# Weight tiles of an encoder kernel stored interleaved in pairs and loaded with a step of 8 bytes

## The chip, the core and the metric

The kernel runs on one core of one Trainium2 chip. The time is device microseconds of one execution of the whole program. TensorE (PE) has two granted clocks here, 1.2 and 2.4 GHz; the profile writes them as 0.5 and 1.00. PEld in the profile is TensorE's weight load (LDWEIGHTS), PE its matmul.

## The reference

One step of a streaming encoder of two layers, for 512 new frames and 64 frames of a running stream, 576 columns (tokens) in all, with a model width of 1024:

```
for i in range(2):
    x = x + 0.5 * swiglu(rmsnorm(x), ffn1_w_in[i], ffn1_w_out[i])      # 1024 -> 2 x 2816 -> 1024
    u = rmsnorm(x)
    y = pool_mixer(u) if i == 0 else mlstm_mixer(u)                    # causal pooling / matrix memory
    x = x + y
    x = x + 0.5 * swiglu(rmsnorm(x), ffn2_w_in[i], ffn2_w_out[i])
y = rmsnorm(x)
```

Beside y the states of both mixers are returned. All inputs are float32. The four SwiGLU blocks are nearly all of the arithmetic.

## The kernel before

**The products.** Every large product is done as three float32r matmuls of one weight tile of 128x128: high part of the weights by high part of the data, high by low, low by high. `passes(u, kk, m_h, m_l)` (L1829) gives these three pairs in this order for tile `kk` of unit `u`. The matmul's stationary operand, which PEld loads, is the weight tile: 128 partitions, 128 float32 columns. The moving operand is 288 columns of data, half of the 576 tokens (`HALF`). No load serves two matmuls: each matmul has its own LDWEIGHTS of 128 columns, issued as the matmul ahead of it starts.

**Four FFNs, each in two phases.** In a phase `ffn_in` runs the products into the hidden layer (`product_mm`, matmuls recorded at L1850), 77 products of 4 tiles x 3 passes on sums and differences of the blocks, held in `u7`; then `ffn_out` runs the products back (`block_mm`, recorded at L1840), 8 output tiles of 11 weight tiles x 3 passes x 2 halves on `h_hi` and `h_lo`. The mLSTM projections (`project`) use `block_mm` too, on `um_hi` and `um_lo`.

**The weights' way.** A DMA brings a unit into a raw buffer (`raw_x`, `raw_y`, `raw_z`, `w_raw`, ...). ACT copies it rounded to float32r into `w_hi` (L726), DVE writes the remainder into `w_lo` (L1231), both contiguous, at `PLACE[u]` in a ring of 8 entries of 4 tiles (2048 bytes in a partition). PE frees an entry by `unit_used`. Of the units of an output tile one has 6 weight tiles and one 5 (`OUT_UNIT`); the pool mixer reads its weights as moving operand (L2032), and the gates are a unit of their own.

**Addresses in a partition.** From the sizes in the code, taken modulo 256 bytes: `w_hi` 128 (address 120192), `w_lo` 128 (136576), the high pieces of `u7` 0 and the low pieces 128, `h_hi`, `h_lo`, `um_hi`, `um_lo` 0 at the first half and 128 at the second, since a half is 1152 bytes, 4.5 times 256. A weight tile is 512 bytes, so every tile begins at its tensor's residue.

Of the kernel before, what the change touches and what calls it, by code (L numbers as in the profile page):

```python
# [3 lines left out]
P = 128  # L4
D_MODEL = 1024
DT = D_MODEL // P
# [5 lines left out]
FT = D_FF // P  # L12
PAIRS = FT // 2
# [13 lines left out]
ENTRY = 4 * P  # L27
RING = 8
OUT_UNIT = (6, 5)
# [101 lines left out]
AT, KEYS, PLACE, LEAVES, RAW_AFTER, SLOT, TURN = unit_tables()  # L131
# [3 lines left out]
def encoder_step(nc, a):  # L135
    F32, F32R = mybir.dt.float32, mybir.dt.float32r
# [5 lines left out]
    def region(size):  # L142
        offset = place[0]
        place[0] += (size + 63) // 64 * 64
        assert place[0] <= nc.sbuf_usable_end, place[0]
        return offset

    def sb(name, shape, dt=F32, at=None):
        size = 4
        for s in shape[1:]:  # L150
            size *= s
        return nc.alloc_sbuf_tensor_at(name, shape, dt, offset=region(size) if at is None else at)
# [4 lines left out]
    def align(size, residue=0):  # L157
        place[0] += (residue - place[0]) % size
# [18 lines left out]
    raw_z = [sb(f"raw_z{s}", [P, ENTRY], at=raw_at + (2 + s) * ENTRY * 4) for s in range(2)]  # L177
    raw_y = [sb(f"raw_y{s}", [P, ENTRY], at=raw_at + (4 + 2 * s) * ENTRY * 4) for s in range(2)]
    raw_x = [sb(f"raw_x{s}", [P, ENTRY], at=raw_at + (5 + 2 * s) * ENTRY * 4) for s in range(2)]
    w_hi, w_lo = sb("w_hi", [P, RING * ENTRY], F32R), sb("w_lo", [P, RING * ENTRY], F32R)  # L180
    rstd = sb("rstd", [P, TOK])
    rows_at = region(4 * TOK * 4)
    tmp = sb("tmp", [P, 2, TOK], at=rows_at)
# [240 lines left out]
    with block as block:  # L424
# [111 lines left out]
        def _(pool):  # L536
# [122 lines left out]
            for c in range(NB):  # L659
                _, n = block_cols(c)  # L660
                pool.wait_ge(scale_ready, c // 2 + 1)
                pool.tensor_tensor(v_one[0:n, c, :, 0:DV], v_one[0:n, c, :, 0:DV],
                                   dd[0:n, c, :].unsqueeze(2).to_broadcast([n, HEADS, DV]), ALU.mult) \
                    .then_inc(h_scaled, 1)
# [15 lines left out]
        def _(act):  # L680
# [403 lines left out]
            for j in range(DT):  # L1084
                middle, _ = IN_O[j]
                if j == 5:
                    variance_root(1)
                if middle and middle[0] == "vt":
                    item("vt", 7, ITEM_AT[8])
                elif middle:  # L1090
                    c = middle[1]
                    _, L = block_cols(c)
                    act.wait_ge(out_read, c + 1)
                    for h in range(HEADS):
                        last = act.activation(junk[0:L, :], v_one[0:L, c, h, 0:DV], ACT.Square,
                                              accum_out=ssum[0:L, c, h:h + 1])
                        if h < HEADS - 1:
                            last.then_inc(act_order, 1)
                            order += 1
                            act.wait_ge(act_order, order)  # L1100
                    last.then_inc(squares, 1)
                if j == 3:
                    variance_root(0)
                if j < DT - 1:
                    ahead(U_M + 17 + j)
                else:
                    y_high(0)
                if j == 5:
                    variance_root(2)
                act.wait_ge(proj_read, 18 + j + 1)  # L1110
                act.activation(og[:, j, :], og[:, j, :], ACT.Sigmoid).then_inc(og_ready, 1)
# [92 lines left out]
        def _(dve):  # L1204
# [451 lines left out]
            def chunk(kind, c):  # L1656

                _, L = block_cols(c)
                old, new = old_state(c)
                if kind == "upd":  # L1660
                    dve.wait_ge(upd_psum, c + 1)
                    if c == 0:
                        dve.wait_ge(q_scaled, NB - 1)
                        dve.tensor_copy(c_st[new][:, :, :], ps[:, 4:8, 0:DV + 1]).then_inc(state_ready, 1)
                        return
                    if c == NB - 1:
                        dve.wait_ge(state_landed, 16)
                    else:
                        dve.wait_ge(state_ready, c)
                    for h in range(HEADS):  # L1670
                        last = dve.scalar_tensor_tensor(
                            c_st[new][:, h, :], c_st[old][:, h, :],
                            carry[:, c - 1:c, h], ps[:, 4 + h, 0:DV + 1], ALU.mult, ALU.add)
                    last.then_inc(state_ready, 1)
                elif kind == "out":
                    dve.wait_ge(out_psum, c + 1)
                    dve.tensor_copy(v_one[0:L, c, :, :], ps[0:L, 4:8, 0:DV + 1]).then_inc(out_read, 1)
# [150 lines left out]

        @block.tensor  # L1829
        def _(pe):  # L1830
            def passes(u, kk, m_h, m_l):

                w = slice(PLACE[u] + kk * P, PLACE[u] + (kk + 1) * P)
                return (w_hi[:, w], m_h), (w_hi[:, w], m_l), (w_lo[:, w], m_h)

            def block_mm(u, kk, k, bank, first, last):

                for p, (w, m) in enumerate(passes(u, kk, *k)):
                    for h in range(2):
                        mm = pe.matmul(ps[:, bank + h, 0:HALF], w, m[:, h * HALF:(h + 1) * HALF],  # L1840
                                       start=first and p == 0, stop=last and p == 2)
                return mm

            def product_mm(f, ph, prod, n, kp):

                u = f.unit(ph, prod, n)
                dst = r_bank(n) if prod in ("M5", "M3") else q_bank(f, ph, n) if prod == "M2" else p_bank(n)
                piece = PIECES.index(MOVING[prod])
                for p, (w, m) in enumerate(passes(u, kp, u7[:, kp, piece, 0, :], u7[:, kp, piece, 1, :])):
                    mm = pe.matmul(dst, w, m, start=prod in ("M1", "M2", "M5") and kp == 0 and p == 0,  # L1850
                                   stop=kp == KP - 1 and p == 2,
                                   skip_group_check=prod in ("M3", "M4", "M6", "M7"))
                if kp == KP - 1:
                    mm.then_inc(unit_used, 1)
# [371 lines left out]
            def last_half(h, first, end):  # L2226

                at = slice(h * HALF, (h + 1) * HALF)
                for k in range(first, end):
                    s, kk = (0, k) if k < OUT_UNIT[0] else (1, k - OUT_UNIT[0])  # L2230
                    u = ffn_d.unit(1, "out", DT - 1, s)
                    for p, (w, m) in enumerate(passes(u, kk, h_hi[:, k, at], h_lo[:, k, at])):
                        mm = pe.matmul(ps[:, out_bank(DT - 1) + h, 0:HALF], w, m, start=k == 0 and p == 0,  # L2233
                                       stop=k == PAIRS - 1 and p == 2, skip_group_check=True)
                if end == PAIRS:
                    mm.then_inc(half_out, 1)
# [128 lines left out]
```

## Time and profile before

| | |
|---|---|
| time, median of 3 runs | 1878.55 us (1876.36 to 1881.43) |
| the profiled execution | 1879.91 us, its span 1878.1 us |
| mean granted TensorE clock | 0.996 |
| PE, PEld busy | 99%, 98% of the span |
| DVE, ACT, POOL busy | 67%, 46%, 18% |
| DMA | 234.71 MB, 125 GB/s mean |

Matmuls overlap in the records: one of 288 columns is recorded as about 295 ns long, while the next starts after about 130 ns. So the record's length is not what one costs; the distance between starts is. It is read here from the timeline, where rows of matmuls alternate in their operands, or as a stretch divided by the matmuls that start in it.

### The profile page before, as it was taken

The numbers are of one execution on the slowest core, as the hardware profiler recorded it, in microseconds if no ns is written. First come the engines' busy times: TensorE is split into PE (matmuls) and PEld (weight loads), VectorE is DVE, ScalarE is ACT, GpSimd is POOL, SyncE is SP. The second block draws the span as 40 slices with busy tenths as digits, with TensorE's granted clock in tenths as the row PEclk, the third lists the DMA queues.
The fourth block names the chain that finished last, engine by engine and source line by source line (L and its number), as shares of the span: only waits on it lengthen the run. The fifth ranks groups of instructions, "written<-read, shape, count | busy, mean of one in ns | idle before, by whom it ended". The sixth has DMA issues, their size and how long they took to land.

```text
span 1878.1 us, 34441 instructions
## 1 busy us (share of the span) xinstructions
PE 1855.2 (99%) x13850; PEld 1834.6 (98%) x13850; DVE 1251.5 (67%) x1999; ACT 866.9 (46%) x1518; POOL 329.5 (18%) x352
## 2 busy tenths in 40 slices
PE   8999999999999999999999999999999999999998
PEld 8999999998999999999999999999989999999998
DVE  7874487668884488679853886563546888548853
ACT  7552355347552355346532553232334665235532
POOL 2220122131220122132201221300010322012112
PEclk9999999999999999999999999999999999999999
DMA  8773576334763576347644763231113576357632
GB/s 207 166 149 105 128 167 148 108 85 95 166 147 108 127 167 150 107 107 165 146 131 102 171 141 101 86 102 68 57 45 103 117 169 152 108 120 167 135 93 82
DMA packets 116830, 234.71 MB, mean 125 GB/s; under 512 B 13184, under 2 KB 15248, under 8 KB 116672
## 3 DMA queue, kind: packets, MB, share of 16 engines
q1 hardware_dynamic: 77440, 160.59, 28.7%
q0 software_dynamic: 38208, 69.42, 22.5%
q8 instruction: 111, 1.82, 0.4%
q10 hardware_dynamic: 1024, 2.49, 0.4%
q14 instruction: 47, 0.39, 0.1%
HBM read 228.92 MB, written 3.53 MB: 124 GB/s over the span
## 4 chain that ended last, share of the span: by engine, by line
PE 93%; DVE 4%; ACT 2%; DMA 1%; issue 1%; DVEq 0%; ACTq 0%
PE ps L1850 49%; PE ps L1840 39%; DVE w_lo L1231 1%; PE ps L1895 1%; PE ps L2167 1%; PE ps L2233 0%; DVE u L1285 0%; DMA raw_z<-in_ffn_in 0%; PE ps L2170 0%; DMA x<-in_x 0%; PE ps L2032 0%; PE ps L2157 0%; DVE rstd L1302 0%; ACT w_hi L726 0%; PE ps L2142 0%
## 5 line engine op out<-in xcount | busy, mean ns | idle before, releaser
L1850 PE MATMUL ps<-u,w_hi 128*128 128x288 f32 x4928 | 984.0, 295 | 11.7 <-DVE w_lo L1231 4.5
L1850 PEld LDWEIGHTS ps<-u,w_hi 128*128 128x128 f32 x4928 | 790.6, 188 | 16.4 <-DVE w_lo L1231 9.4
L1850 PE MATMUL ps<-u,w_lo 128*128 128x288 f32 x2464 | 727.1, 295 | 0.0
L1850 PEld LDWEIGHTS ps<-u,w_lo 128*128 128x128 f32 x2464 | 462.6, 188 | 0.0
L1840 PE MATMUL ps<-h_hi,w_hi 128*128 128x288 f32 x1386 | 294.4, 293 | 0.0
L1840 PE MATMUL ps<-h_lo,w_hi 128*128 128x288 f32 x1386 | 294.3, 293 | 0.0
L1840 PE MATMUL ps<-h_hi,w_lo 128*128 128x288 f32 x1386 | 294.3, 293 | 0.0
L726 ACT ACTIVATE w_hi<-w_raw 128x768 fp32r<-128x768 f32 (+3 forms) x164 | 136.0, 836 | 316.6 <-PE ps L1840 240.2
L1231 DVE TENSOR_TENSOR w_lo<-w_raw,w_hi 128x768 fp32r<-128x768 f32 (+3 forms) x164 | 168.8, 1038 | 160.6 <-ACT w_hi L726 158.4
L1840 PEld LDWEIGHTS ps<-h_hi,w_lo 128*128 128x128 f32 x1386 | 220.4, 188 | 0.0
L1840 PEld LDWEIGHTS ps<-h_hi,w_hi 128*128 128x128 f32 x1386 | 220.3, 188 | 0.0
L1840 PEld LDWEIGHTS ps<-h_lo,w_hi 128*128 128x128 f32 x1386 | 220.3, 188 | 0.0
L588 POOL DMA_DIRECT2D raw_y<-in_ffn_in x88 | 76.0, 872 | 794.3 <-DVE raw_z L1237 786.3
L726 ACT ACTIVATE w_hi<-raw_y 128x512 fp32r<-128x512 f32 x176 | 109.5, 630 | 181.1 <-DMA raw_y<-in_ffn_in 70.7
L726 ACT ACTIVATE w_hi<-raw_z 128x512 fp32r<-128x512 f32 x176 | 111.0, 632 | 108.6 <-PE ps L1850 55.2
L1231 DVE TENSOR_TENSOR w_lo<-raw_z,w_hi 128x512 fp32r<-128x512 f32 x176 | 121.0, 688 | 51.1 <-ACT w_hi L726 50.9
L1231 DVE TENSOR_TENSOR w_lo<-raw_y,w_hi 128x512 fp32r<-128x512 f32 x176 | 122.6, 698 | 42.9 <-ACT w_hi L726 38.9
L1840 PE MATMUL ps<-um_hi,w_hi 128*128 128x288 f32 x512 | 114.8, 305 | 0.6 <-DVE q_t L1584 0.3
L1231 DVE TENSOR_TENSOR w_lo<-raw_a,w_hi 128x512 fp32r<-128x512 f32 x132 | 90.7, 687 | 34.3 <-ACT w_hi L726 34.2
L580 POOL DMA_DIRECT2D raw_x<-in_ffn_in x88 | 92.2, 1048 | 104.5 <-DMA raw_x<-in_ffn_in 103.0
L1840 PE MATMUL ps<-um_lo,w_hi 128*128 128x288 f32 x512 | 110.5, 297 | 0.0
L1840 PE MATMUL ps<-um_hi,w_lo 128*128 128x288 f32 x512 | 110.4, 297 | 0.0
(268 smaller groups left out, 2123.5 us busy)
## 6 DMA issues: line engine op xcount, KB each, us to landing
raw_a<-in_ffn_in SPq DMA_DIRECT2D x132, 256.0 KB, 4.2
w_raw<-in_ffn_out SPq DMA_DIRECT2D x64, 384.0 KB, 3.2
raw_y<-in_ffn_in SPq DMA_DIRECT2D x88, 256.0 KB, 3.6
raw_x<-in_ffn_in SPq DMA_DIRECT2D x88, 256.0 KB, 2.7
raw_x<-in_ffn_in POOLq DMA_DIRECT2D x88, 256.0 KB, 6.5
raw_y<-in_ffn_in POOLq DMA_DIRECT2D x88, 256.0 KB, 4.9
raw_z<-in_ffn_in POOLq DMA_DIRECT2D x88, 256.0 KB, 5.1
w_raw<-in_ffn_out SPq DMA_DIRECT2D x64, 320.0 KB, 3.0
```

The lines of the kernel that those rows point to most:

```text
L580: pool.dma_start(raw_x[g % 2][:, :], f.w_in[ph * PAIRS + n, 3, :, :], accum_op=ALU.add) \
L588: pool.dma_start(raw_y[g % 2][:, :], f.w_in[ph * PAIRS + n, 2, :, :], accum_op=ALU.add) \
L726: act.activation(w_hi[:, PLACE[u]:PLACE[u] + cols], src, ACT.Copy).then_inc(hi_split, 1)
L1231: dve.tensor_tensor(w_lo[:, PLACE[u]:PLACE[u] + cols], src, f32(w_hi[:, PLACE[u]:PLACE[u] + cols]), ALU.subtract).then_inc(lo_split, 1)
L1840: mm = pe.matmul(ps[:, bank + h, 0:HALF], w, m[:, h * HALF:(h + 1) * HALF], start=first and p == 0, stop=last and p == 2)
L1850: mm = pe.matmul(dst, w, m, start=prod in ("M1", "M2", "M5") and kp == 0 and p == 0, stop=kp == KP - 1 and p == 2, skip_group_check=prod i ...
L1895: mm = pe.matmul(ps[:, 6 + h, 0:HALF], mean_w[:, :], sq8[:, j, h * HALF:(h + 1) * HALF], start=i == 0, stop=i == DT - 1, skip_group_check= ...
L2167: mm = pe.matmul(ps[0:L, 4 + h, 0:DV + 1], probs[0:L, h, c0:c0 + L], v_one[0:L, c, h, :], start=True, stop=c == 0)
```

## The change

Four things change, all of them data layout. (1) On the host two neighbouring weight tiles of each unit are interleaved column by column: column 0 of the first, column 0 of the second, column 1 of the first, and so on. The eleventh tile of an output column has no partner and stays as it was. The pool's and the gates' weights stay too. (2) PE loads a tile of a pair with a step of two floats, 8 bytes, over 1024 bytes; the odd tile of a pair begins 4 bytes further. (3) `w_hi` is aligned to residue 128 of 256, where it already was, and `w_lo` to residue 0, 128 bytes further than it was. (4) What is allocated behind `w_lo` moves by 128 bytes with it, so that `h_hi` and `h_lo` begin at residue 128 and their second halves at 0; `u7`, `um_hi` and `um_lo` stay. The halves of 288 columns stay. Each engine's instructions, their order and their waits are the same in both kernels.

```
-    w_hi, w_lo = sb("w_hi", [P, RING * ENTRY], F32R), sb("w_lo", [P, RING * ENTRY], F32R)
+    align(256, 128)
+    w_hi = sb("w_hi", [P, RING * ENTRY], F32R)
+    align(256)
+    w_lo = sb("w_lo", [P, RING * ENTRY], F32R)
...
+            def tile_of(ring, u, kk):
+
+                if KEYS[u][2:3] == ("out",) and KEYS[u][4] == 1 and kk == OUT_UNIT[1] - 1:
+                    return ring[:, PLACE[u] + kk * P:PLACE[u] + (kk + 1) * P]
+                at = PLACE[u] + kk // 2 * 2 * P
+                return ring[:, at:at + 2 * P].rearrange("p (m two) -> p two m", two=2)[:, kk % 2]
+
             def passes(u, kk, m_h, m_l):
 
-                w = slice(PLACE[u] + kk * P, PLACE[u] + (kk + 1) * P)
-                return (w_hi[:, w], m_h), (w_hi[:, w], m_l), (w_lo[:, w], m_h)
+                w_h, w_l = tile_of(w_hi, u, kk), tile_of(w_lo, u, kk)
+                return (w_h, m_h), (w_h, m_l), (w_l, m_h)
...
+    def paired(w):
+
+        return w.reshape(w.shape[:-1] + (-1, 2, P)).swapaxes(-2, -1).reshape(w.shape)
+
     def ffn_in(w):
         w = np.asarray(w).reshape(2, KP, 2, P, 2, FT, P).transpose(0, 5, 4, 2, 3, 1, 6)
-        return w.reshape(2, FT, 4, P, ENTRY)
+        return paired(w.reshape(2, FT, 4, P, ENTRY))
 
     def ffn_out(w):
-        return np.asarray(w).reshape(2, FT, P, DT, P).transpose(0, 3, 2, 1, 4).reshape(2, DT, P, FT * P)
+        w = np.asarray(w).reshape(2, FT, P, DT, P).transpose(0, 3, 2, 1, 4).reshape(2, DT, P, 2, PAIRS * P)
+        even = (PAIRS - 1) * P
+        return np.concatenate([paired(w[..., :even]), w[..., even:]], -1).reshape(2, DT, P, FT * P)
 
     def square_w(w, n):
-        return np.asarray(w).reshape(DT, P, n, P).transpose(2, 1, 0, 3).reshape(n, P, DT * P)
+        return paired(np.asarray(w).reshape(DT, P, n, P).transpose(2, 1, 0, 3).reshape(n, P, DT * P))
```

## Rows read from the trace of the kernel before

**Rows 1.** The page, busy time of each engine: busy us (share of the span) xinstructions.

```profile
PE 1855.2 (99%) x13850; PEld 1834.6 (98%) x13850; DVE 1251.5 (67%) x1999; ACT 866.9 (46%) x1518; POOL 329.5 (18%) x352
```

**Rows 2.** The page, the chain of work that ended last, by engine and by line.

```profile
PE 93%; DVE 4%; ACT 2%; DMA 1%; issue 1%; DVEq 0%; ACTq 0%
PE ps L1850 49%; PE ps L1840 39%; DVE w_lo L1231 1%; PE ps L1895 1%; PE ps L2167 1%; PE ps L2233 0%; DVE u L1285 0%; DMA raw_z<-in_ffn_in 0%; PE ps L2170 0%; DMA x<-in_x 0%; PE ps L2032 0%; PE ps L2157 0%; DVE rstd L1302 0%; ACT w_hi L726 0%; PE ps L2142 0%
```

**Rows 3.** Groups by line and form, PE: xcount | busy us, mean ns | idle before.

```profile
L1850 PE MATMUL ps<-u,w_hi 128*128 128x288 f32 x4928 | 984.0, 295 | 11.7 <-DVE w_lo L1231 4.5 <-DVE u L1285 3.5 <-DVE tmp L1325 1.7
L1850 PE MATMUL ps<-u,w_lo 128*128 128x288 f32 x2464 | 727.1, 295 | 0.0
L1840 PE MATMUL ps<-h_hi,w_hi 128*128 128x288 f32 x1386 | 294.4, 293 | 0.0
...
L1840 PE MATMUL ps<-um_hi,w_hi 128*128 128x288 f32 x512 | 114.8, 305 | 0.6 <-DVE q_t L1584 0.3 <-DVE og L1316 0.2
```

**Rows 4.** Windows: start:end, length, busy us (xinstructions) of each engine, clock, DMA.

```profile
core 0: us, PE busy (x) PEld busy (x) DVE busy (x) ACT busy (x) POOL busy (x), PEclk, DMA share, GB/s
60.00:130.00 70.00, 70.00 (x531) 70.00 (x531) 59.50 (x103) 41.11 (x77) 16.37 (x19) 1.00 0.71 153
150.00:205.00 55.00, 55.00 (x426) 55.00 (x425) 19.57 (x25) 12.55 (x18) 0.00 (x0) 1.00 0.32 94
220.00:320.00 100.00, 100.00 (x758) 100.00 (x758) 81.00 (x139) 57.25 (x108) 22.69 (x26) 1.00 0.72 157
340.00:400.00 60.00, 60.00 (x453) 60.00 (x452) 37.31 (x48) 21.08 (x30) 14.04 (x11) 1.00 0.34 99
850.00:950.00 100.00, 100.00 (x765) 100.00 (x764) 83.03 (x144) 56.95 (x106) 22.58 (x26) 1.00 0.75 163
1500.00:1600.00 100.00, 100.00 (x758) 100.00 (x758) 83.86 (x144) 58.03 (x107) 22.65 (x26) 1.00 0.74 166
```

**Rows 5.** Timeline of PE from 17.6 us: start us, length us, then what.

```profile
17.63 0.85 PE L1850 MATMUL ps<-u,w_hi 128*128 128x288 f32 x2 [3.17 <-DVE w_lo L1231]
18.27 0.44 PE L1850 MATMUL ps<-u,w_lo 128*128 128x288 f32 x1
18.51 0.68 PE L1850 MATMUL ps<-u,w_hi 128*128 128x288 f32 x2
18.99 0.44 PE L1850 MATMUL ps<-u,w_lo 128*128 128x288 f32 x1
```

**Rows 6.** Windows, the granted clock of that stretch.

```profile
17.00:20.00 3.00, 2.37 (x10) 2.37 (x11) 3.00 (x5) 2.14 (x5) 0.86 (x1) 0.50 0.23 51
28.00:29.00 1.00, 1.00 (x7) 0.84 (x6) 1.00 (x3) 1.00 (x2) 0.00 (x0) 1.00 0.93 162
```

**Rows 7.** Timeline of PE, the float32 matmuls of a norm.

```profile
27.51 1.38 PE L1895 MATMUL ps<-sq,mean_w 128*128 128x288 f32 x5
```

**Rows 8.** One line, L1895: durations ns min/median/max.

```profile
L1895 PE MATMUL ps<-sq,mean_w x64: 403/406/407, 26.8 to 460.0; 128*128 128x288 f32 x64
```

**Rows 9.** One line, L1840: durations ns min/median/max of load and matmul.

```profile
L1840 PEld LDWEIGHTS ps<-h_hi,w_lo x1386: 187/187/192, 148.4 to 1857.8; 128*128 128x128 f32 x198
L1840 PE MATMUL ps<-h_hi,w_lo x1386: 291/292/302, 148.5 to 1857.9; 128*128 128x288 f32 x198
```

**Rows 10.** Timeline of PE at a pause in the stream.

```profile
328.91 0.43 PE L1850 MATMUL ps<-u,w_hi 128*128 128x288 f32 x2
329.18 0.29 PE L1850 MATMUL ps<-u,w_lo 128*128 128x288 f32 x1
330.10 0.50 PE L1850 MATMUL ps<-u,w_hi 128*128 128x288 f32 x2 [0.63 <-ACT side L804]
```

**Rows 11.** Timeline of PEld at the same pause.

```profile
329.05 0.19 PEld L1850 LDWEIGHTS ps<-u,w_lo 128*128 128x128 f32 x1
330.07 0.30 PEld L1850 LDWEIGHTS ps<-u,w_hi 128*128 128x128 f32 x2 [0.84 <-DVE w_lo L1231]
330.31 0.19 PEld L1850 LDWEIGHTS ps<-u,w_lo 128*128 128x128 f32 x1
```

**Rows 12.** Waits, longest in total first: us, times, longest.

```profile
DVE w_lo L1231 <- ACT w_hi L726: 318.2, 279, 4.2
ACT w_hi L726 <- PE ps L1840: 303.9, 93, 7.2
...
ACT w_hi L726 <- PE ps L1850: 136.4, 163, 2.4
```

## The prediction

> **What bounds the kernel now.** I read the page's busy line first: PE is busy 99% and PEld 98% of the span [rows 1]. Then the chain that ended last: 93% of it is PE, 49% at L1850 (in-products) and 39% at L1840 (out-products and projections) [rows 2]. No wait can give much: PE's idle time at L1850 is 11.7 us in all [rows 3]. So only the cost of one matmul matters. There are 4928 + 2464 = 7392 at L1850 and, with three passes of 1386 on h and three of 512 on um, 5694 at L1840 [rows 3], 13086 in all.
>
> What one costs is read from stretches [rows 4]. A stretch counts each matmul that touches it; at 0.29 us of length and a distance of 0.13 us that is about 2.2 more than it has room for. In-products: 70 us / (531 - 2.2) = 132.4 ns, 100 / (758 - 2.2) = 132.3, and 131.1 in the stretch at 850 (765). Out-products: 55 / (426 - 2.2) = 129.8 at 150 and 60 / (453 - 2.2) = 133.1 at 340, with the same instructions. I use 132.1 for L1850 and 131.4 for L1840. 288 columns at 2.4 GHz are 120 ns. So 11 to 12 ns of each matmul, some 150 us of the run, is something else. The change can only act on that, or on the load.
>
> **What is in the 12 ns.** Three rows bound it. At the 1.2 GHz clock (granted clock 0.50 in that stretch [rows 6]; PE had just stood idle 3.17 us) three matmuls take 18.99 - 18.27 = 0.72 us [rows 5], 240 ns each: exactly 288 / 1.2, nothing added. The norm's float32 matmuls run at the full clock but take two clocks a column: five in 1.38 us, each 0.406 long [rows 7, 8], so (1.38 - 0.406) / 4 = 0.243 us, 3 ns over 576 / 2.4 = 240. Both have a load of 128 columns beside each matmul; both read the moving data at half speed. The addition thus appears where float32r data is read at full speed. And it isn't one number: equal code at equal residues runs at 129.8 in one out-stage and 133.1 in another, and the maxima stretch together: a load of 187 ns goes to 192, a matmul of 292 to 302 [rows 9]. That is what two readers in each other's way look like. It would come from addresses: moving data passes 4 bytes each 0.42 ns, 9.6 bytes/ns; the load takes about 0.30 - 0.19 = 0.11 us for its 512 bytes after a pause [rows 11], 4.7 bytes/ns. The faster stream overtakes the other again and again.
>
> **The change, part by part.**
> - Step of 8 bytes: a load now passes 1024 bytes in the same 0.11 us, 9.3 bytes/ns, nearly the moving data's speed. The two keep their distance instead of lapping.
> - Residues, L1850: the load beside each matmul is the next pass's. High data (0) beside a high load (128), low data (128) beside a low load (0), high data (0) beside the next high load (128): always 128 bytes apart modulo 256. Before, the second pair was 0 apart.
> - Residues, L1840: halves alternate between 0 and 128 while the tensor stays, so of six pairs three are 128 apart and three 0, for h and for um, whether the tile begins at 128 (h now) or 0 (um). Before it was three and three too.
> - Host interleaving: nothing in device time; DMA, ACT and DVE move the same contiguous bytes. No instruction or wait moves. DVE's remainders wait 318.2 us for ACT, and ACT 303.9 + 136.4 us for PE [rows 12]: the supply has slack. If PE got 7% faster, DVE would go from 84% [rows 4] to 90% in the in-stages: still cover, and the next limit after that.
> - Moving what lies behind w_lo by 128 bytes: bound by what one residue or another gives now, between 129.8 and 133.1 on the out-stages.
>
> **The sum.** If keeping apart removes all that the half-speed rows don't have, a matmul costs 123 ns (120 + 3): 9.1 x 7392 = 67 us at L1850 and 8.4 x 5694 = 48 us at L1840, together 115 us; with only half of the L1840 pairs freed, 91 us. At the other end nothing is removed. One row holds me back from the full value. The last matmul before a pause has no load beside it, its successor's load comes at 330.07, 0.9 us later [rows 11], yet it is recorded 0.29 long like all others [rows 10]. Ends are modelled, so the row is weak, but it says that a part of the 12 ns isn't the load's. I take half: L1850 to 127.5 ns, 4.6 x 7392 = 34 us; L1840, where half of the pairs coincide, a quarter, 2.1 x 5694 = 12 us. From the profiled execution, 1879.9 - 46 = 1834; the median lies 1.4 us lower: **1832 us**.
>
> The Trainium skill speaks on both sides. SBUF — State Buffer, section Specifications, says that SBUF is read in lines of 16 bytes and wants at least two hits on a line: a float32 step of 8 bytes has exactly two, so by that rule the load keeps its pace, which no row here shows for a weight load.
>
> **The rivals.**
> - *No change.* The 12 ns are a cost of reading float32r at full speed whatever lies beside, as the matmul before the pause suggests [rows 10]. Then the load's step and residue touch nothing and the time is 1879 us, 1873 to 1884. Against it: the unequal stages and the load that stretches with its matmul [rows 4, 9]. The Trainium skill, TensorE: Matmul & The Clock Gate, section Part 2: What happens when you issue a matmul, gives TensorE two independent read ports, so that a load takes nothing from the running matmul; by it this case would hold.
> - *Slower by contact.* A load now touches twice as many lines (64 of 16 bytes instead of 32) in the same time. Where a pair coincides, three of six at L1840, equal speed means that it stays in contact over the whole load instead of passing through. It decides if a contact costs the matmul a fixed time and neither stream gives way for good. If it leaves all stages in the worst state seen, 133.3 ns, it costs 1.2 x 7392 + 1.9 x 5694 = 20 us: 1898. If the added time doubles at the coinciding half of L1840, 12 x 2847 = 34 us more, 1932, less whatever L1850 gives back.
> - *The load becomes the bound.* If a step of 8 bytes halves the load's rate, 0.11 us becomes 0.22 and that, not the 120 ns, sets the distance: about 88 x 13086 = 1150 us more, 3030 us. It begins to decide when the load takes longer than 0.13 us, a fifth more than now. Nothing in the trace shows a strided load, for or against.
> - *The supply becomes the bound.* With PE faster, DVE at 90% would cap the gain only below about 120 ns a matmul; it changes no sign.
>
> **How the numbers follow.** Forecast case (the streams keep apart, part or all of it recovered, 1764 to 1872): 0.54. No change: 0.17. Slower by contact, 1885 to 1935: 0.24. Load-bound: 0.05. About 0.3% (5.6 us) is what a measurement of this kernel can tell from no change. The forecast case's low tail near 1764 has little weight; I leave out what is below 1770, the upper part of the contact case and the load-bound one, together about 0.2: 1770 to 1900. Forecast case alone: 1775 to 1868. A few hundredths of it fall within 0.3%, and a few of no change outside: faster 0.53, same 0.18, slower 0.29.
>
> **What would show it.** Right: stretches of the in-stages hold about 784 matmuls in 100 us instead of 758, the out-stages gain less, loads stay at 187 ns, and the span of PE's idle time doesn't grow. No-change: the same counts as now. Contact: L1850 faster or equal, L1840 slower, with loads above 192 ns. Load-bound: loads recorded near 290 ns and starts over 200 ns apart. The forecast is wrong in its basis if the loads' length and the residues turn out to have nothing to do with the added 12 ns.

## The result: slower by 0.9%, and the profile after

| | before | after |
|---|---|---|
| median | 1879.51 us (1876.36 to 1881.43, 4 runs) | 1895.99 us (1892.68 to 1897.24, 4 runs) |
| ratio | 1 | 1.0087, 95% interval 1.0066 to 1.0107 |
| span of the profiled execution | 1878.1 us | 1895.4 us |

Measured again on another occasion, with four more runs, the changed kernel stood at 1.0060 (1.0043 to 1.0077) of the kernel before, 1893.1 against 1880.9 us. It is slower either way. The forecast was 1832 us.

The page's busy line and the chain of the changed kernel answer [rows 1, 2]. L1850 and L1840 have become L1860 and L1850:

```profile
PE 1872.3 (99%) x13850; PEld 1851.6 (98%) x13850; DVE 1253.2 (66%) x1999; ACT 867.8 (46%) x1518; POOL 329.5 (17%) x352
...
PE 92%; DVE 4%; ACT 2%; DMA 1%; issue 1%; DVEq 0%; ACTq 0%
PE ps L1860 49%; PE ps L1850 39%; DMA raw_y<-in_ffn_in 1%; DVE w_lo L1234 1%; DVE u L1288 1%; PE ps L2177 1%; PE ps L2243 0%; ACT w_hi L729 0%; PE ps L2180 0%; DMA x<-in_x 0%; PE ps L2167 0%; PE ps L2042 0%; PE ps L2152 0%; ACT u L771 0%; DVE rstd L1299 0%
```

The shape is the same and PE's busy time is 17.1 us longer: no new wait, the matmuls themselves stand further apart. The windows of the changed kernel, columns as in [rows 4] but PE alone:

```profile
60.00:130.00 70.00, 70.00 (x527) 1.00 0.67 150
150.00:205.00 55.00, 55.00 (x416) 1.00 0.32 96
220.00:320.00 100.00, 100.00 (x752) 1.00 0.72 160
345.00:395.00 50.00, 50.00 (x379) 1.00 0.35 101
860.00:940.00 80.00, 80.00 (x602) 1.00 0.75 165
1040.00:1140.00 100.00, 100.00 (x752) 1.00 0.71 155
```

By the prediction's own count, 100 us / (752 - 2.2) = 133.4 ns in the in-products and 55 / (416 - 2.2) = 132.9 in the out-products. The load's recorded length moved too. Lines of the changed kernel, durations in ns min/median/max, to be held against [rows 9]:

```profile
L1860 PEld LDWEIGHTS ps<-u,w_lo x2464: 192/195/334, 8.7 to 1813.7; 128*128 128x128 f32 x190
...
L1850 PEld LDWEIGHTS ps<-h_hi,w_lo x1386: 187/197/201, 149.0 to 1875.1; 128*128 128x128 f32 x198
L1850 PE MATMUL ps<-h_hi,w_lo x1386: 288/296/299, 149.1 to 1875.2; 128*128 128x288 f32 x198
```

Loads went from 187 to 195 or 197, far from the 290 of a load at half rate. The stretches can be read finer than by windows: the starts of the single matmuls in the trace, over the 500 to 900 that follow one another in a stage without a pause, give mean distances that are the same in one stage after another. I call the eight stretches of in-products in-stages, the eight of FFN out-products out-stages, and such a mean the distance to which a stage settles. In the kernel before only four values occur: 131.11 and 132.22 ns in in-stages, 130.0 and 133.33 in out-stages. In the changed kernel every in-stage is at 133.33 and every out-stage at 132.76 to 132.79.

**Where the time went.** Over all neighbours less than 200 ns apart the mean went from 132.09 to 133.35 ns at the in-products, 1.26 x 7392 = 9.3 us, and from 131.42 to 132.75 at the out-products and projections, 1.33 x 5694 = 7.6 us. Together 16.9 of the 17.3 us between the two profiled spans.

### The profile page after: what moved, and what is told of

Its sections match the earlier page's. It is cut to its first block, busy times and chain, and to the rows that moved or that the text cites. A ratio compares the mean times of both kernels' runs of the same rounds, so it can differ in the third digit from the quotient of the medians.

```text
span 1895.4 us, 34441 instructions
## 1 busy us (share of the span) xinstructions
PE 1872.3 (99%) x13850; PEld 1851.6 (98%) x13850; DVE 1253.2 (66%) x1999; ACT 867.8 (46%) x1518; POOL 329.5 (17%) x352
## 3 DMA queue, kind: packets, MB, share of 16 engines
q10 hardware_dynamic: 1024, 2.49, 0.4%
## 4 chain that ended last, share of the span: by engine, by line
PE 92%; DVE 4%; ACT 2%; DMA 1%; issue 1%; DVEq 0%; ACTq 0%
PE ps L1860 49%; PE ps L1850 39%; DMA raw_y<-in_ffn_in 1%; DVE w_lo L1234 1%; DVE u L1288 1%; PE ps L2177 1%; PE ps L2243 0%; ACT w_hi L729 0%; PE ps L2180 0%; DMA x<-in_x 0%; PE ps L2167 0%; PE ps L2042 0%; PE ps L2152 0%; ACT u L771 0%; DVE rstd L1299 0%
## 5 line engine op out<-in xcount | busy, mean ns | idle before, releaser
L1860 PE MATMUL ps<-u,w_hi 128*128 128x288 f32 x4928 | 993.4, 297 | 11.9 <-DVE u L1288 3.9
L1860 PEld LDWEIGHTS ps<-u,w_hi 128*128 128x128 f32 x4928 | 817.3, 196 | 16.9 <-DVE w_lo L1234 9.6
L1860 PE MATMUL ps<-u,w_lo 128*128 128x288 f32 x2464 | 734.6, 298 | 0.0
L1860 PEld LDWEIGHTS ps<-u,w_lo 128*128 128x128 f32 x2464 | 481.4, 195 | 0.0
L1850 PE MATMUL ps<-h_hi,w_lo 128*128 128x288 f32 x1386 | 297.2, 296 | 0.0
L1850 PE MATMUL ps<-h_hi,w_hi 128*128 128x288 f32 x1386 | 297.0, 296 | 0.0
L1850 PE MATMUL ps<-h_lo,w_hi 128*128 128x288 f32 x1386 | 296.4, 296 | 0.0
L1850 PEld LDWEIGHTS ps<-h_hi,w_lo 128*128 128x128 f32 x1386 | 228.4, 196 | 0.0
L1850 PEld LDWEIGHTS ps<-h_lo,w_hi 128*128 128x128 f32 x1386 | 227.7, 195 | 0.0
L1850 PEld LDWEIGHTS ps<-h_hi,w_hi 128*128 128x128 f32 x1386 | 227.4, 195 | 0.0
L1850 PE MATMUL ps<-um_hi,w_hi 128*128 128x288 f32 x512 | 114.5, 305 | 0.6 <-DVE q_t L1587 0.4
L1850 PE MATMUL ps<-um_lo,w_hi 128*128 128x288 f32 x512 | 110.6, 297 | 0.0
L1850 PE MATMUL ps<-um_hi,w_lo 128*128 128x288 f32 x512 | 109.9, 296 | 0.0
```

## The experiments

The theories at the start: the step costs (twice as many lines a load, in the matmul's way); the distance between load and moving data costs; the residues alone cost and the step is innocent. Settled distances below are from the starts in each trace. Kernels were run in several sittings, and the kernel before took 1878.7 to 1884.9 us in them (medians or single runs), so each time is to be held against the kernel before beside it.

| kernel | time, us | before beside it, us | in-stages, ns | FFN out-stages, ns | load, ns (mean at the in-products) |
|---|---|---|---|---|---|
| before, first profile | 1879.5 | | 132.2 (one 131.1) | 130.0, two 133.3 | 188 |
| changed | 1896.0 | 1879.5 | 133.3 | 132.8 | 196 |
| pairs_only | 1894.2 | 1882.0 | 133.3 | 132.5 | 196 |
| residue_only | 1894.8 | 1882.0 | 133.3 | 133.0 | 188 |
| pairs_d0 | 1894.7 | 1882.0 | 133.3 | 132.8 | 195 |
| pairs_d64 | 1896.1, one run | 1884.9 | 133.3 | 133.3 | 196 |
| w_at_0 | 1889.8 | 1884.9 | 132.2 | 133.3 | 189 |
| w_at_64 | 1885.0, one run | 1884.9 | 132.6 (last 132.2) | 132.2 | 189 |
| short_loads | 1874.8, one run | 1882.0 | 131.1 | 131.7 | 152 |
| pairs_short | 1874.6, one run | 1881.1, one run | 131.1 | 131.5 | 156 |
| short32 | 1875.3, one run | 1878.7, one run | 133.3, the first 130.0 | 130.0 | 135 |

### One part at a time: pairs_only and residue_only

pairs_only keeps the interleaving and the step, and puts `w_lo` back:

```
-    align(256)
     w_lo = sb("w_lo", [P, RING * ENTRY], F32R)
```

> The step of 8 bytes alone: w_lo and all behind it stay where they were before (residue 128, h at 0). If the step costs the time (each load touches twice as many lines), the in-stages run at 133.3 ns a matmul as in the changed kernel, loads are recorded near 196 ns instead of 188, and the time is 1890 to 1900 us. If the residues cost it, the time is within 4 us of before, 1879.

residue_only keeps the contiguous loads of before and moves `w_lo` and all behind it by 128 bytes (two small tensors go into the gap):

```
+    align(256, 0)
     w_lo = sb("w_lo", [P, RING * ENTRY], F32R)
```

> The residues alone: w_lo 128 bytes further and what lies behind it moved, weights read contiguously. If the step costs the time, this one stays at 1879, give or take the 4 states of 130.0 to 133.3 ns that the stages of before already show (1870 to 1890), with loads at 188 ns. If the residues cost it, 1896 and the in-stages at 133.3 ns.

1894.2 us, ratio 1.0059 (1.0042 to 1.0076), and 1894.8 us, 1.0064 (1.0048 to 1.0079). Each part alone costs as much as can be told from both: neither theory had that. In-stages of both, at 220 or 650 us, first pairs_only, then residue_only:

```profile
220.00:320.00 100.00, 100.00 (x752) 1.00 0.74 159
650.00:750.00 100.00, 100.00 (x752) 1.00 0.73 156
```

```profile
220.00:320.00 100.00, 100.00 (x752) 1.00 0.75 160
650.00:750.00 100.00, 100.00 (x753) 1.00 0.72 155
```

752 in both, as in the changed kernel. But the loads tell them apart, pairs_only first, then residue_only:

```profile
L1858 PEld LDWEIGHTS ps<-u,w_lo x2464: 192/196/330, 8.7 to 1811.4; 128*128 128x128 f32 x190
```

```profile
L1852 PEld LDWEIGHTS ps<-u,w_lo x2464: 186/188/331, 8.6 to 1811.5; 128*128 128x128 f32 x190
```

So the 7 to 8 ns of the load belong to the step alone, and the matmuls come to 133.33 ns with or without them. The two costs don't add: in the in-products both end at the same distance. In the mLSTM projections neither does: there pairs_only settled at 131.7 or 133.3 ns and residue_only at 132.2 or 130.0, in the changed kernel 132.2 or 132.8. residue_only also moves the buffers of other engines behind `w_lo`; the two weight tensors at unlike residues with all else in place was not run.

### The steady distance: pairs_d0 and pairs_d64

The step of 8 bytes as in the change, with `w_hi` and `w_lo` at residues 0 and 128, or 64 and 192; small tensors fill the gaps, so that everything behind stands at the residues of before.

```
-    align(256, 128)
+    align(256, 0)
     w_hi = sb("w_hi", [P, RING * ENTRY], F32R)
-    align(256)
+    align(256, 128)
     w_lo = sb("w_lo", [P, RING * ENTRY], F32R)
+    align(256, 128)
```

> The step of 8 bytes with w_hi at residue 0 and w_lo at 128, so that at the in-products each load begins 0 bytes modulo 256 from the moving data beside it, always; h at 0. If a steady distance matters (the idea behind my forecast), this is the worst case at L1860: well over 133.3 ns, 1920 or more, since the changed kernel with distance 128 has 133.3. If only the doubled lines matter, about the changed kernel's 1896. If the sign is the other way round, under 1880.

> Step of 8 bytes, loads always 64 bytes modulo 256 from the moving data at the in-products. Distances 0 and 128 both gave 133.3 ns. If the steady distance has no part in it, 133.3 again and 1894 us; if the streams touch at 0 and at 128 but not between, under 130 ns and under 1850.

1894.7 us (ratio 1.0072, 1.0051 to 1.0092) and 1896.1. In-products at steady distances 0, 64 and 128 (the changed kernel) all settle at 133.33 ns, and so do those of pairs_only, where the distance alternates. So under the step the distance between load and moving data makes no difference at the in-products. That takes the ground from the forecast.

### Contiguous loads at other residues: w_at_0 and w_at_64

The kernel before with both weight tensors at residue 0, or both at 64, filled up in the same way.

> Contiguous loads, both weight tensors at residue 0 instead of 128, all other large tensors at the residues of before. In-products: each load 0, 128, 0 from its moving data instead of 128, 0, 128. If the distance of load and moving data sets the time, the in-stages change from 132.2 ns: to about 130 if distance 0 is the cheap one, as 128.9 against 132.8 at the two halves of the out-stages of before hints, so 1865 us; if it is only that the two weight tensors must be alike, 1879. If neither, 133.3 ns and 1895 us.

> The same with both weight tensors at residue 64. If what counts is a distance modulo 256, this lies between residue 0 and 128; if what counts is that both are alike, in-stages stay at 131 to 132.2 ns. One look: 1870 to 1897 us.

w_at_0: 1889.8 us, 1.0027 (1.0012 to 1.0041). In-stages keep 132.2 ns, as the "alike" reading had it, but all eight out-stages of its one profile are at 133.3. At 64 there are two other values, 132.6 in the in-stages and 132.2 in the out-stages, at a time that is the kernel before's. Residues thus select which distances a stage can settle to. That 130.0 can't occur with the weights at 0 is not shown by one profile, though the time of seven runs fits with it.

### Less load: short_loads, short32 and pairs_short

Second and third pass with 64 (or 32) weight columns; only the first 64 (32) result rows get them, so these matmuls also write fewer rows of PSUM, which was not tried by itself. The first two are the kernel before, pairs_short has the step of 8 bytes:

```
-                return (w_hi[:, w], m_h), (w_hi[:, w], m_l), (w_lo[:, w], m_h)
+                n = slice(PLACE[u] + kk * P, PLACE[u] + kk * P + P // 2)
+                return (w_hi[:, w], m_h), (w_hi[:, n], m_l), (w_lo[:, n], m_h)
```

> Kernel before with the second and third pass of every product at 64 weight columns instead of 128: their half of the result rows gets only the first pass, so that part of the product is left out. Loads of these passes read half as long, 288 moving columns stay. If the 12 ns over 120 come from the load beside the matmul, the matmuls that have a short load beside them (two of three) lose about half of it, 6 ns: mean 128 ns, about 1825 us. If they are a cost of the moving data's own reading, the distance stays 130 to 133 ns and the time 1879.

> Kernel before with 32 weight columns in the second and third pass (three quarters of the result rows lack these passes). With 64 columns the in-stages were at 131.1 ns. If the remaining 11 ns have anything to do with how long the load reads, they fall again, to 128 or less. If they are the moving data's own, 131.1 stays.

> The step of 8 bytes with w_lo where it was, and 64 weight columns in the second and third pass (their half of the result rows lacks these passes). If the step's 1.1 ns come from the load's doubled lines beside the matmul, halving two of three loads brings the in-stages from 133.3 to between 131.1 (what short contiguous loads gave) and 132.5; 1876 to 1888 us. If the step's cost is in how a load starts or ends beside the matmul's start, 133.3 and 1893.

The load of `w_lo` in short_loads and in pairs_short:

```profile
L1853 PEld LDWEIGHTS ps<-u,w_lo x2464: 133/134/224, 8.8 to 1791.9; 128*64 128x64 f32 x190
```

```profile
L1859 PEld LDWEIGHTS ps<-u,w_lo x2464: 135/137/223, 8.6 to 1791.8; 128*64 128x64 f32 x190
```

and short_loads' windows:

```profile
220.00:320.00 100.00, 100.00 (x765) 1.00 0.72 158
345.00:395.00 50.00, 50.00 (x382) 1.00 0.34 101
```

Two of three loads are 53 ns shorter, yet the matmuls only come to 131.1 and 131.7 ns, one run of 1874.8 us. 131.1 is a value that full loads have too, in one in-stage of the kernel before. With 32 columns seven in-stages are at 133.3 and the out-stages at 130.0. So of the 12 ns over 120 at least 10 stay however short these loads are: the prediction's "half of it is the load's" is wrong. Each matmul still has a load of its own in all these kernels; a cost per load that doesn't depend on its length is left open, and a matmul without a load was not tried. pairs_short answers the other question. With the step, full loads gave 133.33 in every in-stage; short loads give 131.11, what short contiguous ones give. The step's cost therefore does pass through the reading of a full load: in the in-products it takes away the settled distances below 133.33 and no more.

### What else the 11 ns could be: overwrite, cols272, cols512, bf16_pass

overwrite sets `start=True` in every matmul of the in-products, the out-products and the projections, save the 66 of the last output tile (L2233 of the kernel before), so that nothing is added up in PSUM. The edit at the out-products:

```
-                                       start=first and p == 0, stop=last and p == 2)
+                                       start=True, stop=last and p == 2, skip_group_check=True)
```

> Kernel before, every matmul overwrites its bank instead of adding to it; the result is that of the last pass alone. If the 10 to 13 ns over 120 come from adding in PSUM at full speed, matmuls fall to 122 to 125 ns and the time to about 1780 us. If PSUM has no part in it, the states of before, 130.0 to 133.3 ns, and 1879.

1882.1 us. Distances are those of before: in-stages 131.1 or 132.2, out-stages 130.0 twice and 133.3 six times. So PSUM's adding has no part. It was also the first trace in which stages of the same code at the same addresses settled elsewhere than in the profile of before.

cols272 reads 272 of 288 columns at the out-products and projections, in all matmuls but the first of each half of an output tile:

```
-                        mm = pe.matmul(ps[:, bank + h, 0:HALF], w, m[:, h * HALF:(h + 1) * HALF],
+                        n = HALF if first and p == 0 else 272
+                        mm = pe.matmul(ps[:, bank + h, 0:n], w, m[:, h * HALF:h * HALF + n],
```

> Kernel before with 272 instead of 288 moving columns in all but the first pass of the out-products and projections (the last 16 columns of each half get the first pass only). A cost fixed per matmul gives 113.3 + 10 to 13.3 = 123.3 to 126.7 ns; one in proportion to the columns 122.8 to 125.9. What it can tell better is whether distances still come in whole units of 3.33 ns over a repeating group: 10.0 over 113.3 exactly, or 13.3, and the same loads beside them.

1841.7 us, one run, against 1881.1. Out-stages settle at two distances again:

```profile
345.00:395.00 50.00, 50.00 (x402) 1.00 0.37 103
1130.00:1180.00 50.00, 50.00 (x407) 1.00 0.31 89
```

Some ten matmuls after the last that keeps 288 columns, the starts are 125.00 ns apart on average in six of the eight out-stages and 123.33 in the other two, and stay so to the end of the output tile (two of the six have one output tile at 123.33). They repeat in groups of four (124, 125, 128, 123 ns) and of two (121 or 122, and 125): 500.0 and 246.7 ns, whole multiples of 3.33 ns as in the kernel before. The lower distance is 10.0 over 113.3, as 130.0 is 10.0 over 120: the expectation's sign of a fixed addition, where one in proportion would give 122.8. The higher one is 11.7 over, not 13.3, and fits neither.

> Out-products and projections with 512 moving columns into one bank and 64 into the other instead of 288 and 288; the tokens end in other places, so the result isn't the reference's, and part of the second bank gets only the first pass. It tells what the addition is to: if it is a fixed cost of a matmul, 512 columns take 213.3 + 10 to 13 = 223 to 227 ns; if it grows with the columns (10 to 11%), 235 to 237 ns. If it came from the load beside it, which is over after 107 ns either way, also a fixed 10 to 13.

The edit is `n = 512 if h == 0 else HALF if first and p == 0 else 64`; 2105.1 us, one run. Each pair of a 512 and a 64 column matmul takes 0.34 us. If the short one is bound by the load of its successor, 0.11 us by [rows 11], about 0.23 is left for 512 columns, an estimate: some 17 ns over 213. The 0.11 is known to 0.01 us only, so this reaches to both expectations and doesn't decide between them.

> Like the overwriting kernel, but the second of three passes takes its moving data as bfloat16: 288 columns of 2 bytes, half the bytes a column at the same 2.4 GHz; weights as the upper halves of w_hi; the pass's product is overwritten. If the 11 ns belong to reading 4 bytes a column at full speed, this pass takes about 122 to 123 ns and the mean of three falls from 131.5 to about 128.5, 1845 us. If they are a cost of any matmul at full clock, nothing falls.

The second pass reads `m_l.bitcast(BF)` with `w_hi`'s upper halves. Timeline of PE in the in-products:

```profile
99.82 0.43 PE L1853 MATMUL ps<-u,w_hi 128*128 128x288 f32 x2
100.00 0.39 PE L1853 MATMUL ps<-u,w_lo 128*128 128x288 f32 x1
100.23 0.43 PE L1853 MATMUL ps<-u,w_hi 128*128 128x288 f32 x2
100.40 0.39 PE L1853 MATMUL ps<-u,w_lo 128*128 128x288 f32 x1
```

Starts of these rows come 0.17 and 0.23 us apart instead of 0.27 and 0.13, and three passes take 0.40 us, no less than before; the one run took 1891.2 us against 1878.7. Alternating the type may cost something itself, which was not tried apart, so the run doesn't answer the question.

### The sequence of residues: same_moving, order, halves_outer

same_moving reads `m_h` in the second pass too (the pass on `m_l` is left out), so the moving data is always at residue 0:

```
+                return (w_hi[:, w], m_h), (w_hi[:, w], m_h), (w_lo[:, w], m_h)
```

> Kernel before with the high moving data in the second pass again instead of the low; that pass's product is left out of the result. In-products then always read moving data at residue 0 with loads at 128. If a distance of 128 is the dear one and 0 the cheap one (132.8 against 128.9 in the out-stages of before), the in-stages rise from 132.2 to 133.3 and the time to about 1887. If the moving data's own changes of residue cost something, they fall below 131. The out-stages keep their states.

In-stages at 133.33 ns, all of them; 1897.1 us. Of the out-stages, whose operands stand where they stood before, one is at 130.0 and seven at 133.3. An in-stage, and the out-stage at 130.0:

```profile
230.00:310.00 80.00, 80.00 (x602) 1.00 0.74 162
580.00:630.00 50.00, 50.00 (x387) 1.00 0.35 103
```

> Kernel before with the three passes of one half before those of the other in the out-products and projections: moving residues 0, 0, 0, 128, 128, 128 instead of 0, 128 in turn. Repeating residue 0 gave 133.3 ns in the in-products. If a change of residue is what lets a group end early, these stages go to about 133.3 or between it and 130, 1880 to 1890 us; if residue 128 against loads at 128 is the cheap pair whatever went before, they come to about 130 (133.3 and 127 mixed).

With `for h in range(2):` outside the passes, out-stages settle at 133.3 and never at 130.0; in-stages keep 132.2; 1887.5 us. In both profiles no stage whose moving residue is repeated three times or more settles below 133.33. For the in-products that is clear, since seven profiles of kernels with contiguous full loads and both weight tensors at residue 128 or at 0 (before, before_again, overwrite, cols272, order, halves_outer, w_at_0) have none at 133.33 there. For the out-products it is weaker: same_moving, where they still take turns, had 130.0 only once in eight.

> Kernel before with the passes in the order high-high, low-high, high-low: moving residues 0, 0, 128 instead of 0, 128, 0 at the in-products, which over the repeating group is the same cycle, shifted; loads always at 128. If only the sequence of residues counts, the in-stages stay at 131.1 or 132.2 ns and the out-stages too: 1870 to 1890 us. Anything else says that w_hi and w_lo differ by more than their residue.

`(w_hi, m_h), (w_lo, m_h), (w_hi, m_l)`: 1881.5 us, in-stages at 131.1 or 132.2, out-stages at 130.0 three times, 133.3 five times. The out-products of this kernel read the same residues as before, so their other mixture is not the order's doing.

### The same kernels again: before_again and after_again

> The kernel before, unchanged, profiled a second time. If a stage's state is drawn in each execution, the out-stages at 130.0 and at 133.3 ns and the in-stages at 131.1 and 132.2 are others than in the first profile, and no stage has another value. If the state follows from addresses and history alone, stage by stage the same as in the first profile. Time within 0.3% of before either way.

> The changed kernel, unchanged, profiled a second time: in-stages at 133.33 ns and out-stages at 132.8 as in its first profile, 1892 to 1898 us. If its stages too are drawn, some come to 131.1 or 130.0.

before_again took 1880.2 us (ratio to before 0.9999, 0.9989 to 1.0008). Its windows:

```profile
60.00:130.00 70.00, 70.00 (x536) 1.00 0.69 154
150.00:205.00 55.00, 55.00 (x415) 1.00 0.32 94
...
340.00:400.00 60.00, 60.00 (x464) 1.00 0.33 97
...
650.00:750.00 100.00, 100.00 (x765) 1.00 0.74 160
```

536 against 531 and 415 against 426 [rows 4]: the first in-stage settled at 131.1 where it had been at 132.2, the first out-stage at 133.3 where it had been at 130.0, and at 340 us the other way round (464 against 453). Over the eight FFN phases 130.0 now stands three times in the out-stages, and had stood six times; 131.1 stands four times in the in-stages, and had stood once. So the distance isn't a property of the stage: it differs from one execution of the same program to another. I call it a draw. The two profiles are of different sittings, so that the sitting makes the difference isn't excluded by them; but within one sitting ten runs of the kernel before ranged from 1877.6 to 1890.1 us, and seven of w_at_0 from 1887.7 to 1893.7.

after_again took 1893.1 us; all its in-stages are at 133.33 and its FFN out-stages at 132.8, as in the first profile. Only its last projections are elsewhere, 132.8 ns against 132.2. So in its FFNs the changed kernel shows no draw, and still its runs differ by up to 6 us. The granted clock has a part in that. Around 473 and 1306 us of the first profile it fell, in the second it didn't; first after, then after_again:

```profile
473.00:477.00 4.00, 4.00 (x20) 0.57 0.32 77
1306.00:1310.00 4.00, 4.00 (x19) 0.57 0.38 130
```

```profile
473.00:477.00 4.00, 3.66 (x28) 1.00 0.00 0
1306.00:1310.00 4.00, 4.00 (x32) 1.00 0.39 131
```

By the traces the first profile spent 6.8 us more at granted clock 0.5, which costs 3.4 of the 3.7 us between the two spans (1895.4 and 1891.7).

## Why the prediction failed, point by point

**What bounds the kernel: right.** PE's stream sets the time, and 11 to 12 ns a matmul lie above 120. The change acted on these alone.

**What is in the 12 ns: the step that failed.** The prediction took the vanishing of the addition at half speed, the unequal stages and a load that stretches with its matmul for a sign of two streams lapping. The half-speed rows show only that the addition goes when the moving data is read at half the rate, not that it needs a load. Loads half or a quarter as long, and steady distances of 0, 64 and 128, left 10 ns or more of it. The row that had held the forecast back, the matmul before a pause that is as long as all others without a load beside it [rows 10], pointed the right way; with modelled ends it can't show more. The term that was wrong is the half that was taken to be the load's. The sum's 4.6 ns at the in-products measured -1.3, its 2.1 at the out-products -1.3.

**Reading one profile's stages.** 129.8 and 133.1 ns with equal code was read as a property of the stages and as a bound for the moved addresses. It is a draw. Its right use was as a warning: something in the present layout lets stages settle low, and the change can lose it. That is what happened: the change keeps all in-stages at 133.33 and gives none of the out-stages 130.0.

**Residues.** "Between 129.8 and 133.1" for what moves held as a range (132.8), but the residue of `w_lo` was costed as a gain. With contiguous loads, and what lies behind it moved too (residue_only), it takes the in-stages from 132.2 to 133.3.

**Step.** The load slowed from 187 to 195 ns, not to 290; the rival of the load as the bound didn't come. By the Trainium skill, SBUF — State Buffer, section Specifications, two hits on a line of 16 bytes keep full bandwidth; the trace agrees but for 7 to 8 ns of the 187 recorded. From 64 to 128 columns a contiguous load grows by 53 ns (134 to 187) and one with the step by 58 (137 to 195): 0.83 and 0.91 ns a column, 9% more, which the page's rule doesn't have.

**The rivals.** "Slower by contact", 1898 us, stood for 133.3 ns in all stages, and 1896 was measured. Its size was right, and so was its sign of loads above 192 ns, and that full loads with the step are one way to get there (pairs_short). That the number was met is in part luck: residue_only comes to the same 133.3 ns without the step, and pairs_d0 and pairs_d64 show no effect of where a load meets the moving data. Its place was wrong as well: the coinciding half of the out-products was to suffer, and these are at 132.8 while the in-products, never coinciding, are at 133.3. "No change" was right in that most of the 12 ns doesn't depend on the load's length, step or residue, and wrong in that loads have no effect at all: with 128, 64 and 32 columns in two of three loads the in-stages were mostly at 132.2, 131.1 and 133.3 ns, with the step at 133.3. The page TensorE: Matmul & The Clock Gate of the Trainium skill, section Part 2: What happens when you issue a matmul, has the two read ports independent; these runs agree to within such 1 to 2 ns a matmul, and a shorter load doesn't always mean a shorter distance.

**The supply: right.** ACT waits longer for PE in the changed kernel, 320.3 us for the out-products and projections (now L1850) and 157.0 for the in-products (L1860), against 303.9 and 136.4 [rows 12]:

```profile
ACT w_hi L729 <- PE ps L1850: 320.3, 98, 7.2
...
ACT w_hi L729 <- PE ps L1860: 157.0, 228, 2.8
```

**What stays open.** What the 10 or 11 ns are. They don't come from the load's length, the distance of load and moving data, or the adding in PSUM; they go at half speed, and the 10.0 are the same for 272 and 288 columns. A fixed cost of having a load at all, and a cost of reading float32r, both remain. Why a group of matmuls settles on one of two distances, and by what the residues select them, wasn't found. Moving data at other residues than 0 and 128 wasn't tried. No version tried beats the kernel before: the four under its time (short_loads, pairs_short, short32, cols272) leave out part of the products.

## What to carry to other kernels

When equal stretches of code run at a few exact, different distances, profile the same kernel twice before explaining them: what changes from one execution to the next isn't a property of the code, and an average over executions is what an edit must beat. Before designing against a suspected conflict, shrink one of its two parties; here halving the load would have shown in one run that most of the addition doesn't depend on how long the load reads. An edit of addresses can lose time where nothing waits, because a layout may have been allowing the fast ones of several distances.

## What the runs showed of the hardware

- In the FFN stages of the kernel before (float32r matmuls of 288 columns at 2.4 GHz, weights at residue 128) the mean distance is one of 130.00, 131.11, 132.22 and 133.33 ns. The single distances repeat in groups of 2, 3, 6 and 4 matmuls (132 and 128 ns; 133, 127, 133), and the groups are whole multiples of 3.33 ns (260, 393.3, 793.3, 533.3). At 1.2 GHz it is 240 ns with nothing over 288 / 1.2 [rows 5].
- With 272 columns the distances are 123.33 and 125.00 ns (cols272), again whole multiples over groups of 2 and 4.
- Which of them a stage takes differs between executions of the kernel before. Out-stages at 130.0 or at 133.3 differ by 3.3 x about 530 = 1.8 us each, in-stages by 1.1 x about 840 = 0.9; eight of each can move the time by some 20 us, by my estimate. Its runs ranged from 1876 to 1890 us, the granted clock's share included.
- A step of 8 bytes lengthens the recorded load of 128 float32r columns from 187 to 195 ns, and one of 64 columns from 134 to 137.
- Loads of 64 or 32 instead of 128 columns beside two of three matmuls leave the distance of the FFN stages between 130.0 and 133.3 ns.
